# Moving two modulation vectors from the second attention to the query projection and the first expert chunks

## The reference

```python
# first block, one layer
mod = jnp.einsum('bd,lde->lbe', jax.nn.silu(c), w_ada) + b_ada[:, None, :]
sh1, sc1, g1, sh2, sc2, g2 = jnp.split(mod[l], 6, axis=-1)
h = modulate(rms_norm(x, norm_attn[l]), sh1, sc1)
x = x + g1[:, None, :] * hybrid_mixer(h, w_in[l], w_out[l], rel_bias)
h = modulate(rms_norm(x, norm_ffn[l]), sh2, sc2)
x = x + g2[:, None, :] * peer_ffn(h, peer_wq[l], peer_subkeys[l], peer_u[l], peer_v[l])

# second block, two layers (NSA attention, then sliding-window attention)
cond = jax.nn.silu(c)
mod = cond @ ada_w[i] + ada_b[i]
sh1, sc1, g1, sh2, sc2, g2 = jnp.split(mod, 6, axis=-1)
h = modulate_2(rms_norm_2(x, norm_g[i, 0]), sh1, sc1)
y = nsa_mixer(...) if i % N_MIXERS == 0 else swa_sink_mixer(...)
x = x + (1 + g1)[:, None, :] * rms_norm_2(y, norm_g[i, 1])
h = modulate_2(rms_norm_2(x, norm_g[i, 2]), sh2, sc2)
y = squared_relu_mlp(h, mlp_w_up[i], mlp_w_down[i])
x = x + (1 + g2)[:, None, :] * rms_norm_2(y, norm_g[i, 3])
```

## Time and profile before

| what | value |
|---|---|
| median of three runs | 1840.32 us |
| the profiled execution's own time | 1842.62 us |
| its span, first to last instruction | 1840.8 us |
| TensorE products, weight loads busy | 93%, 85% |
| VectorE, ScalarE, POOL busy | 66%, 49%, 32% |
| mean granted TensorE clock | 0.951 of full |
| read from HBM | 337.87 MB, 184 GB/s over the span |

### The profile page before, as it was taken

How to read it: one execution, slowest core, us unless ns; L and a number is a source line. 1 busy time by engine, 2 the same in 40 slices (tenths; PEclk the granted TensorE clock), 3 DMA queues, 4 the chain that set the end, 5 groups by cost and what they waited for, 6 DMA issues and landing times.

```text
span 1840.8 us, 32622 instructions
## 1 busy us (share of the span) xinstructions
PE 1720.2 (93%) x11412; PEld 1558.8 (85%) x11412; DVE 1208.5 (66%) x2182; ACT 908.8 (49%) x1705; POOL 593.8 (32%) x240
## 2 busy tenths in 40 slices
PE   2998899999999998999999989998899989779998
PEld 2986799999999997888888779866799979669997
DVE  5456509689538975777787657367378786636665
ACT  2445444455479973455555443166544434554443
POOL 0780577989875553000000027120400014140000
PEclk9999799999999999999999979778899998989999
DMA  8663455555553337788886616332287862125552
GB/s 315 224 209 131 164 167 186 183 181 182 182 160 115 110 123 265 279 291 290 286 294 238 199 56 181 129 127 89 96 282 282 280 236 92 36 95 190 184 186 99
DMA packets 98280, 341.15 MB, mean 185 GB/s; under 512 B 12258, under 2 KB 16114, under 8 KB 98194
## 3 DMA queue, kind: packets, MB, share of 16 engines
q1 hardware_dynamic: 92000, 334.54, 53.6%
q10 hardware_dynamic: 6194, 5.49, 1.0%
HBM read 337.87 MB, written 1.07 MB: 184 GB/s over the span
## 4 chain that ended last, share of the span: by engine, by line
PE 88%; DVE 6%; ACT 2%; DMA 2%; issue 1%; ACTq 1%; SPq 0%; DVEq 0%
PE banks L524 25%; PE banks L525 24%; PE banks L526 24%; PE banks L772 3%; PE banks L591 2%; DMA arena<-in_ada 2%; DVE arena L1351 1%; PE banks L660 1%; PE banks L634 1%; PE banks L910 1%; PE banks L673 1%; PE banks L570 1%; ACT arena L1024 1%; PE banks L639 1%; DVE arena L1443 1%
## 5 line engine op out<-in xcount | busy, mean ns | idle before, releaser
L487 POOL TENSOR_TENSOR weights_low<-ring,weights_high 128x1024 fp32r<-128x1024 f32 x236 | 593.6, 2524 | 1048.6 <-ACT weights_high L983 1048.4
L983 ACT ACTIVATE weights_high<-ring 128x1024 fp32r<-128x1024 f32 x480 | 505.5, 1054 | 531.0 <-PE banks L526 502.4
L524 PE MATMUL banks<-ht_high,weights_high 128*128 128x256 f32 x2008 | 582.9, 290 | 10.2 <-DVE ht_low L1411 7.9
L525 PE MATMUL banks<-ht_low,weights_high 128*128 128x256 f32 x2008 | 572.4, 285 | 0.0
L526 PE MATMUL banks<-ht_high,weights_low 128*128 128x256 f32 x2008 | 572.2, 285 | 0.0
L524 PEld LDWEIGHTS banks<-ht_high,weights_high 128*128 128x128 f32 x2008 | 389.5, 194 | 15.8 <-issue 12.5
L525 PEld LDWEIGHTS banks<-ht_low,weights_high 128*128 128x128 f32 x2008 | 389.9, 194 | 2.8
L526 PEld LDWEIGHTS banks<-ht_high,weights_low 128*128 128x128 f32 x2008 | 389.2, 194 | 0.0
L1678 DVE TENSOR_TENSOR weights_low<-ring,weights_high 128x1024 fp32r<-128x1024 f32 x244 | 295.9, 1222 | 34.5 <-ACT weights_high L983 30.9
L524 PE MATMUL banks<-weights_high,ga_parts 128*128 128x512 f32 x512 | 202.8, 396 | 11.5 <-DVE ga_parts L1673 11.5
L526 PE MATMUL banks<-weights_high,ga_parts 128*128 128x512 f32 x512 | 201.8, 394 | 0.0
(11 more groups left out here) (221 smaller groups left out, 2322.5 us busy)
## 6 DMA issues: line engine op xcount, KB each, us to landing
ring<-in_stream SPq DMA_DIRECT2D x490, 512.0 KB, 3.5
arena<-in_ada SPq DMA_DIRECT2D x88, 512.0 KB, 4.3
ada_ring<-in_ada SPq DMA_DIRECT2D x56, 512.0 KB, 4.3
arena<-bias_rows ACTq DMA_DIRECT2D x1, 2048.0 KB, 7.8
X<-in_x SPq DMA_DIRECT2D x1, 1024.0 KB, 6.3
out<-X SPq DMA_DIRECT2D x2, 512.0 KB, 2.6
arena<-arena ACTq DMA_DIRECT2D x8, 127.5 KB, 5.3
arena<-in_norm_final ACTq DMA_DIRECT2D x1, 512.0 KB, 6.0
```

The costliest lines, as they stand in the source:

```text
L487: pool.tensor_tensor(WL[:, c % SLOTS, :], ring[:, c % SLOTS, :], WH[:, c % HIGHS, :], ALU.subtract)\
L524: pe.matmul(out, wh, xh, start=start, stop=False, **kw)
L525: pe.matmul(out, wh, xl, start=False, stop=False, **kw)
L983: act.activation(WH[:, c % HIGHS, :], ring[:, c % SLOTS, :], ACT.Copy).then_inc(S["high_ready"], 1)
```

## The change

Vector 12 moves beside the expert query projection and vector 13 beside the first expert chunks. In detail:

- SyncE loads the eight pieces of vector 12 between the ring loads of the query projection, into two slots in turn, and those of vector 13 between the next sixteen ring loads, into eight slots (columns 10240 to 18431 of the arena, where the results of expert chunks 40 to 71 come later), without a wait for a free slot. The sixteen loads in the second attention go.
- VectorE adds the pieces of vector 12 after the second norm, before the top 16. It adds those of vector 13 in token tile 0, between the tables and the wait for ScalarE's exponential. The calls in the second attention go.
- TensorE waits for vector 12's sum after the last chunk of the query projection and makes its columns there, before the sub-key products. It makes those of vector 13 after 40 of the 88 plain expert chunks, whose loop becomes two (five and six rounds of eight). The columns after out2 go.
- `mod_columns` for vector 12 stands before the top 16, for vector 13 before the first one-hots; the one after the residual of out2 goes.
- `ADA_BEFORE` and the numbers of the calls follow the new order; the two sums lie at columns 20480 and 21504.

```diff
-A_ACC3 = [A_PHASE, A_WIN] + [A_Q - 512 + i * D for i in range(4)]
+A_ACC3 = [20480, 21504] + [A_Q - 512 + i * D for i in range(4)]
+ADA_WQ, ADA_U = [18432, 19456], [10240 + i * D for i in range(DB)]
-ADA_BEFORE = dict(start=0, qk1=2 * DB, mixer1=3 * DB, out1=4 * DB, peer=5 * DB, layer2=6 * DB, mixer2=12 * DB, mlp2=14 * DB)
+ADA_BEFORE = dict(start=0, qk1=2 * DB, mixer1=3 * DB, out1=4 * DB, wq=5 * DB, u=6 * DB, peer=7 * DB, layer2=8 * DB, mlp2=14 * DB)
@@ SyncE
             ahead = chunk["out1"] + 2 * SLOTS - 1
+            for k in range(DB):
+                load_chunk(ahead + 2 * k)
+                load_ada(k, ADA_WQ, ADA_BEFORE["wq"] + k - 1 if k >= 2 else None, 12 * DB + k, "ada_wq")
+                load_chunk(ahead + 2 * k + 1)
+            ahead += 2 * DB
+            for k in range(DB):
+                load_chunk(ahead + 2 * k)
+                load_ada(k, ADA_U, None, 13 * DB + k, "ada_u")
+                load_chunk(ahead + 2 * k + 1)
+            ahead += 2 * DB
...
             load_chunks(beside + 12 * DB, ahead)
-            for i in range(2 * DB):
-                load_ada(i, ADA_LAYER3, ADA_BEFORE["mixer2"] + i - 1 if i >= 2 else None, 12 * DB + i, "ada3_slot")
@@ TensorE
             product("wq", 16, h_rhs, ready=lambda k: h_ready(1, k))
+            pe.wait_ge(S["ada_used"], ADA_BEFORE["u"])
+            ada_columns([A(A_ACC3[0], D)], 3)
             pe.wait_ge(S["out_taken"], OUTS["wq"] + 16)
...
-            with pe.Fori(0, WOVEN // SLOTS) as r:
-                for s in range(SLOTS):
-                    out = out_bank(o0 + s, r * SLOTS)
-                    chunk_blocks(u0 + s, out, h_rhs, more=r * SLOTS)
+            def plain(first, last):
+                with pe.Fori(first, last) as r:
+                    for s in range(SLOTS):
+                        out = out_bank(o0 + s, r * SLOTS)
+                        chunk_blocks(u0 + s, out, h_rhs, more=r * SLOTS)
+            plain(0, 5)
+            pe.wait_ge(S["ada_used"], ADA_BEFORE["peer"])
+            ada_columns([A(A_ACC3[1], D)], 4)
+            plain(5, WOVEN // SLOTS)
...
             deep("out2", 8, D, ready=lambda k: y_ready(8, k), y=2, rows_after=[(2, 4), (3, 6)])
-            pe.wait_ge(S["ada_used"], ADA_BEFORE["mlp2"])
-            pe.wait_ge(S["gate_rows_taken"], 4)
-            ada_columns([A(first, D) for first in A_ACC3[:2]], 5)
             mlp("2", 3)
@@ VectorE
             norm(1, 1)
             shift_banks(1)
+            for k in range(DB):
+                ada_piece(k, ADA_BEFORE["wq"] + k, "ada_wq", ADA_WQ, A(A_ACC3[0], D), 1)
+            mod_columns(12, 1, 4)
...
                     link(dve.tensor_reduce(picks[t][i], eq, AX, ALU.add))
+                if t == 0:
+                    for k in range(DB):
+                        ada_piece(k, ADA_BEFORE["u"] + k, "ada_u", ADA_U, A(A_ACC3[1], D), 1)
                 dve.wait_ge(S["top_exp"], t + 1)
...
+            mod_columns(13, 1, 5)
             dve.wait_ge(S["pick_taken"], 3)
...
-            def ada_third(step):
-                if step % 3 != 2:
-                    i = step // 3 * 2 + step % 3
-                    ada_piece(i, ADA_BEFORE["mixer2"] + i, "ada3_slot", ADA_LAYER3, A(A_ACC3[i // DB], D), 1)
-            attention(att2, ada_third)
+            attention(att2)
...
             residual2(0)
-            mod_columns(12, 2, 6)
             norm(3, 4)
```

More of the change, by code:

```diff
@@ L414, in load_ada @@
                     a["ada"][bass.ds(more + chunk_of_ada, 1)].rearrange("o p n -> (o p) n")
-                sp.dma_start(A(slots[i % 2], D), src).then_inc(S[f"{landed}{i % 2}"], 16)
+                sp.dma_start(A(slots[i % len(slots)], D), src).then_inc(S[f"{landed}{i % len(slots)}"], 16)
             for c in range(2 * DB):
@@ L735, in _ @@
             deep("out1", 8, D, ready=lambda k: y_ready(0, k), y=0, rows_after=[(0, 4)])
-            pe.wait_ge(S["ada_used"], ADA_BEFORE["peer"])
+            pe.wait_ge(S["ada_used"], ADA_BEFORE["wq"])
             pe.wait_ge(S["gate_rows_taken"], 1)
@@ L805, in _ @@
                     pe.wait_ge(S["ada_used"], ADA_BEFORE["layer2"])
-                    ada_columns([ada_acc[:]], 3)
+                    ada_columns([ada_acc[:]], 5)
             with pe.Fori(0, 6) as r:
@@ L818, in _ @@
             pe.wait_ge(S["ada_used"], ADA_BEFORE["layer2"] + 6 * DB)
-            ada_columns([A(first, D) for first in A_ACC2], 4)
+            ada_columns([A(first, D) for first in A_ACC2], 6)
             def rope(units, u0, raw0, more):
@@ L940, in _ @@
             deep("out2", 8, D, ready=lambda k: y_ready(8, k), y=2, rows_after=[(2, 4), (3, 6)])
-            pe.wait_ge(S["ada_used"], ADA_BEFORE["mlp2"])
-            pe.wait_ge(S["gate_rows_taken"], 4)
-            ada_columns([A(first, D) for first in A_ACC3[:2]], 5)
             mlp("2", 3)
             pe.wait_ge(S["ada_used"], ADA_BEFORE["mlp2"] + 4 * DB)
-            ada_columns([A(first, D) for first in A_ACC3[2:]], 6)
+            ada_columns([A(first, D) for first in A_ACC3[2:]], 7)
             norm_transpose(4)
@@ L1362, in ada_piece @@
             def ada_piece(i, used, landed, slots, acc, layer, more=0, landed_more=0):
-                dve.wait_ge(S[f"{landed}{i % 2}"], landed_more + 16 * (i // 2 + 1))
+                n = len(slots)
+                dve.wait_ge(S[f"{landed}{i % n}"], landed_more + 16 * (i // n + 1))
                 dve.wait_ge(S["ada_used"], more + used)
-                add_ada(i % DB, A(slots[i % 2], D), acc, layer)
+                add_ada(i % DB, A(slots[i % n], D), acc, layer)
             def branch_gates(first):
@@ L1687, in _ @@
                 add_ada(j, ada_ring[:, j % 2, :], ada_acc[:], 0)
-            mod_columns(5, 1, 4)
+            mod_columns(5, 1, 6)
             with dve.Fori(0, 6) as r:
@@ L1756, in rope @@
                     dve.tensor_tensor(dst(i), t1, t2, ALU.add).then_inc(S["rope_done"], 1)
-            mod_columns(6, 6, 5)
+            mod_columns(6, 6, 7)
             branch_gates(2)
@@ L1848, in _ @@
             residual2(1)
-            mod_columns(14, 4, 7)
+            mod_columns(14, 4, 8)
             branch_gates(4)
```

## The result

The changed kernel takes 1845.13 us (median of 20 runs, 1839.41 to 1853.95), the kernel before 1836.37 us on the same chip (20 runs, 1829.74 to 1843.05): ratio 1.0052, 95% interval 1.0039 to 1.0064. It is slower by 8.8 us, 7.2 to 11.8 by the interval. The profiled executions don't show that difference: 1842.47 us after (span 1840.7), near the fast end of its runs, and 1842.62 before, near the slow end of its own. So the traces are compared stage by stage, each from a landmark of its own, not by their ends. Part of what hides the difference lies where nothing was changed: from the first rotations of NSA's projection to the first scores of the second attention the trace before has 101.97 us and the one after 98.99, and a fall of the clock in it lasts 10.2 us in the first and 3.4 in the second.

What follows compares the result with a forecast made beforehand. TensorE was taken to bound the kernel (88% of the last chain), with VectorE nearly full in the second attention. Terms -4.2 - 0.2 + 2.2 + 1.6 + 1.85 + 2.4 = +3.65 gave 1844.0 us, range 1835.5 to 1850.

Steps and rivals of the forecast that it cites:

- the likeliest case: Whole kernel: measured time within 0.3% of the kernel before, chance 0.60.
- Part one: Second attention: sixteen pieces leave VectorE and TensorE becomes the next bound; -4.2 us.
- upper figure of 1.55 a group: Second attention: at most 16.88 - 15.33 = 1.55 us a head group comes free, 6.2 in four.
- VectorE-bound rival: Second attention was bound by VectorE: a group falls to ScalarE's 13.33 us, -14.2 in all; chance 0.08.
- the attention that gets no shorter: Second attention: another wait takes over, 0 instead of -4.2 us, total 1848.2; chance 0.08.
- The clock did not hold all through: Rival judged: clock holds all through the second attention, 4.5 us of falls spared, total 1839.5; chance 0.12.
- Part two: Out2 to mlp2: removing two vectors' columns gives nothing as the norm's chain covers them; one addition gives -0.2 us.
- Part three: End of the query projection, vector 12: wait and columns net +2.2 us, a fall of the clock +1.6.
- two cases in three at 2.4: After the query projection: how the clock's +1.6 us was taken, within bounds of 0 and 2.9.
- Part four: Expert chunks, vector 13: uncovered columns +1.85 us, TensorE waiting for POOL's slowed low parts +2.4.
- the rival's price of 6.3: Expert chunks: POOL becomes the bound, each piece holding it 1.28 us, 8 x 0.79 = 6.3 us; chance 0.17.
- the low parts catch up between pieces: Expert chunks: rival that the moved work is hidden, with no fall of the clock either, 1840; chance 0.13.

Runs made afterwards that it cites:

- only_wq: Changed kernel, but only vector 12 moves, beside the query projection; vector 13's eight pieces stay in the second attention. Ratio 1.0046 to the kernel before.
- paced: Changed kernel, but four of vector 13's additions in VectorE's first pause among the expert chunks, four in its second, columns after chunk 56. Ratio 1.0110 to the kernel before.
- spread: As paced, but vector 13's last four additions stand among VectorE's sub-key searches of the second half. Ratio 1.0011 to the kernel before.
- kept_spread: As sums_kept, with vector 13's additions placed as in spread. 1832.69 us, ratio 0.9979 to the kernel before.
- early_spread: As spread, with vector 12's eight loads also issued sooner, as in early_wq. Ratio 0.9987 to the kernel before.
- the first series: Four kernels run one part at a time: att_free, only_wq, only_u and cols_together. Ratios 0.9989, 1.0046, 1.0036 and 1.0048 to the kernel before.
- att_free: Kernel before, with the second attention's sixteen piece loads and additions left out and put nowhere else; not a usable version. Ratio 0.9989 to the kernel before.
- early_wq: Changed kernel, but vector 12's eight loads are issued sooner, into four places instead of two, none before out1 has ended. Ratio 1.0017 to the kernel before.
- the third series: Runs with the fault of paced mended, among them spread, early_spread and kept_spread, and one_early. Ratios 1.0011, 0.9987, 0.9979 and 1.0002 to the kernel before.
- cols_together: Changed kernel, but vector 12's columns are made together with vector 13's after expert chunk 40; additions stay in place. Ratio 1.0048 to the kernel before.
- sums_kept: As paced, but both sums are stored to HBM, loaded back in the second attention, and columns made between out2 and mlp2. Ratio 1.0075 to the kernel before.
- only_u: Changed kernel, but only vector 13 moves, beside the expert chunks; vector 12 stays in the second attention. Ratio 1.0036 to the kernel before.
- one_early: As only_wq, with vector 12's loads issued sooner as in early_wq; vector 13's eight pieces stay in the second attention. Ratio 1.0002 to the kernel before.

## Why the prediction was right or wrong

The direction and the range held, the likeliest case (no change within 0.3%) did not: forecast +3.65 us, measured +8.8. That the forecast of 1844.0 is only 1.1 us from the measured 1845.13 is luck: it stood on three runs of the kernel before with a median of 1840.32, and twenty have 1836.37. The mechanisms named were found. The clock's price was mis-sized, and about half of the measured loss is in no term. Step by step:

**Part one, -4.2.** Right in mechanism and nearly in size: 4.4 to 4.6 us less. How it comes about is different from the working, which gave the clock only a little. Over the first three groups, from transposes to transposes, it is 17.98 + 16.88 + 19.27 us before and 17.39 + 15.93 + 15.93 after, 4.9 less, and half of that (19.27 - 16.88 = 2.4) is the fall at 1257 that stayed away; the fall at the end lasts longer and takes a little back. The third group by stage, columns as in the earlier trace rows, before and after:
```profile
1248.10:1267.37 19.27, 18.28 (x171) 13.62 (x169) 15.72 (x49) 13.33 (x58) 0.00 (x0) 0.82 0.31 110
```
```profile
1252.48:1268.41 15.93, 15.25 (x171) 11.23 (x169) 11.84 (x44) 13.33 (x58) 0.00 (x0) 1.00 0.00 1
```
The upper figure of 1.55 a group was too high: 15.93 - 15.25 = 0.7 us a group remain in which TensorE waits for others. The VectorE-bound rival falls, with its 13.33 us a group. So does the attention that gets no shorter. The clock did not hold all through, but it fell once less.

**Part two, -0.2.** TensorE's wait before the norm's transposes grew from 5.28 to 8.53 us, as it should when hidden columns go. TensorE's first transposes for the norm, before and after:
```profile
1322.29 3.04 PE L570 MATMUL banks<-const,arena 128*128 128x128 f32 x13 [5.28 <-DVE arena L1391]
```
```profile
1323.59 1.75 PE L579 MATMUL banks<-const,arena 128*128 128x128 f32 x7 [8.53 <-DVE arena L1405]
```
From out2's first transposes to these it is 1322.29 - 1301.62 = 20.7 us before and 1323.59 - 1303.13 = 20.5 after: the 0.2 of the addition, and nothing for the columns. It is part of the 4.6 above.

**Part three, +2.2 for the wait and +1.6 for the clock.** The first is right to the tenth (1.81 of wait; 3.6 - 1.42 = 2.2). The clock's price is the term that was mis-sized. It fell in each of the four traces with wait and columns (the changed kernel, only_wq, paced, spread), and where the sum took 1.6, "two cases in three at 2.4", with 2.9 at worst, it cost 1.6 in the first and 3.2 to 3.4 in the other three: from the last chunk's end to the first expert chunk these are 5.4 to 5.6 us longer than before, 2.2 of them for wait and columns. The columns themselves run slower there too, which the worst case left out.

**Part four, +1.85 and +2.4.** Right: 1.84 and 2.2. The mean low part beside an addition is 3.34 us, as read in out1. The Trainium skill ("SBUF — State Buffer", Who interferes with whom) would have the later instruction blocked for all of the first: a cycle of 3.67 and 4.6 us. The trace doesn't agree in size: the cycle is 3.34 us, 0.33 less than the two alone (2.39 + 1.28), so the two are not wholly one after the other. POOL did become the bound while the pieces lasted, for five or six chunks; the rival's price of 6.3 was too high, and that the low parts catch up between pieces is refuted.

**The sum.** With the measured sizes it is -4.5 + 3.8 + 4.1 = +3.4, or +5.2 with the 5.6 of the other traces for part three, below the 7.2 to 11.8 of the measurement. The terms account for kept_spread (-4.5, measured -3.9), early_spread (-2.6, measured -2.4) and spread (+2.9, measured +2.0); but taking the two new costs away gave 1.0052 - 0.9987 = 12 us, where the terms have 6 to 8. So some 4 to 5 us of the changed kernel's loss, 2 at least, are in no term, and the cause stays open. Three things on record bear on it.

- The same is missing in all four runs of the first series: they lie 2.5 to 5.2 us above their terms, and att_free, which moves nothing, is one of them (-4.5, measured -2.0). So does early_wq in the second, by 3.4. In the third series the three versions that move both vectors lie within 1 us of theirs. Each ratio is uncertain by 4 us or so, and each kernel was run in one series only, so it isn't shown whether the missing part belongs to these kernels or to the series.
- The length of the clock's fall at the end of the second attention: the stretch has 104.4 to 104.9 us in the traces of the changed kernel, att_free, cols_together and sums_kept (fall of 13.7 us), and 100.8 to 101.6 in those of the six others that have no pieces there (3.4 us). With one trace a kernel that is a guess.
- The attention isn't the only stretch that varies. Between the norms around mlp2, where nothing was changed, nine traces have 208.1 to 208.9 us, only_u 214.0 and early_wq 213.1.

## What to carry to other kernels

Before work is moved off a nearly full engine, read the second fullest in the same period: it bounds the gain, and here half the work moved gave less than a quarter of the gain in a group at full clock. Free time of the receiving engine is not enough either: look at which other engine its instructions slow, at the queue on which the new loads stand, and at where the consumer waits. Additions at one in two chunks cost TensorE nothing, eight in a row 2.2 us. The columns were free where the norm hid them, cost 0.1 us behind the projection once the sum was there in time (they took the place of another wait), and 1.84 among the chunks. For a result that isn't needed for long, a store and a load can bring it to a consumer that is covered; that this beats early columns isn't shown, as the intervals overlap.

And a sum of right terms can miss: compare a few executions of each kernel before a difference of two traces is taken for the gain.

## What was not expected of the hardware

- In cols_together the granted clock fell to its lower level in the midst of 32 products of one column among full chunks. It did not at 16 of them (1.84 us; changed kernel and only_u), nor at 16 after the projection without a pause (early_wq, early_spread, one_early). With a pause of 1.8 to 2.0 us before these 16 it did, in four traces of four.
- The lower level lasts for different times in attentions that are written alike, in the traces of different kernels, and so do they: 104.4, 105.2 and 108.2 us with eight pieces, 100.8 to 104.9 without. A stage's length in one trace can't be read to better than 4 us here unless the clock's rows are set beside it.
- Beside each other, VectorE's additions and POOL's low parts both last as long as the common cycle (1.28 to 3.33 us, 2.39 to 3.34). So neither record shows who waits for whom, and neither engine looks idle.
